# Five feed-forward blocks of an fp32 kernel: two-by-two tile schemes with seven products of 128 tokens in place of eight

## The reference, cut to what matters

```python
def swiglu(y, w_gu, w_down):                    # first network, two per layer
    gate, up = jnp.split(y @ w_gu, 2, axis=-1)  # 1024 x 5632
    return (jax.nn.silu(gate) * up) @ w_down    # 2816 x 1024

def half_ffn(h, m, off, g, w_gu, w_down):
    y = modulate(h, g, m[off], m[off + 1])      # RMS norm, scale, shift
    return h + 0.5 * m[off + 2] * swiglu(y, w_gu, w_down)

ffn = _swiglu(x, w_gate, w_up, w_down)          # second network, one per layer
x = _layer_norm(ALPHA * x + ffn, ln2_g, ln2_b)
```

## Time and profile before

| | |
|---|---|
| time, median of 3 runs | 3701.17 us (3699.54 to 3701.4) |
| the profiled execution's own time | 3700.73 us |
| its span (first to last instruction) | 3698.9 us |
| mean granted TensorE clock | 0.967 of full speed |
| PE / PEld / DVE / ACT / POOL busy | 92% / 74% / 28% / 13% / 5% |
| moved by DMA | 459.40 MB |

### The profile page before, as it was taken

One profiled execution on the slowest core, in us unless ns is written; L12 is line 12 of the kernel. 1 busy time (PEld: TensorE's weight loads), 2 busy tenths in 40 slices (PEclk: granted clock), 3 DMA queues, 4 the chain that ended last, 5 costly groups with the idle time before them and its releaser, 6 DMA issues.

```text
span 3698.9 us, 48516 instructions
## 1 busy us (share of the span) xinstructions
PE 3417.8 (92%) x20808; PEld 2727.1 (74%) x20808; DVE 1039.1 (28%) x1893; ACT 483.1 (13%) x835; POOL 185.1 (5%) x262
## 2 busy tenths in 40 slices
PE   3999989789989899899979999999899899999898
PEld 1444435577878688788858878888788788888787
DVE  5533553455665200100330011322100113321101
ACT  1000010233332100100010000111000001120100
POOL 1000100111111000400000000000000000000000
PEclk7999999999999799999989999999999999999999
DMA  7555742100000144444314455233344343324342
GB/s 279 183 203 181 271 182 89 41 6 6 6 9 2 60 156 136 153 149 158 113 57 149 139 182 175 103 136 128 125 136 139 124 148 113 114 97 171 114 141 97
DMA packets 72129, 459.40 MB, mean 124 GB/s; under 512 B 7632, under 2 KB 10320, under 8 KB 26793
## 3 DMA queue, kind: packets, MB, share of 16 engines
q1 hardware_dynamic: 54720, 362.83, 28.4%
q0 software_dynamic: 12192, 87.03, 6.3%
q10 hardware_dynamic: 5065, 7.27, 0.7%
HBM read 451.34 MB, written 5.77 MB: 124 GB/s over the span
## 4 chain that ended last, share of the span: by engine, by line
PE 88%; DVE 8%; ACT 3%; issue 1%; DMA 1%; DVEq 0%; POOL 0%; ACTq 0%; POOLq 0%
PE ps L531 55%; PE ps L945 12%; PE ps L579 3%; PE ps L541 2%; PE ps L550 2%; PE ps L625 1%; PE ps L631 1%; PE ps L612 1%; DVE arena L1413 1%; DVE arena L1742 1%; PE ps L959 1%; PE ps L1009 1%; PE ps L987 1%; PE ps L672 1%; DVE arena L1627 1%
## 5 line engine op out<-in xcount | busy, mean ns | idle before, releaser
L531 PE MATMUL ps<-y,ring 128*128 128x256 f32 (+1 forms) x3520 | 926.0, 426 | 79.9 <-ACT y L1091 66.9
L531 PEld LDWEIGHTS ps<-y,ring 128*128 128x128 f32 x3520 | 677.2, 193 | 328.9 <-issue 231.7
L531 PE MATMUL ps<-arena,ring 128*128 128x256 f32 (+1 forms) x2624 | 643.3, 408 | 7.7 <-DVE arena L1376 6.0
L531 PEld LDWEIGHTS ps<-arena,ring 128*128 128x128 f32 x2624 | 498.1, 190 | 152.7 <-issue 83.7
L531 PE MATMUL ps<-h,ring 128*128 128x256 f32 x2080 | 460.9, 385 | 19.4 <-ACT h L1340 19.4
L531 PEld LDWEIGHTS ps<-h,ring 128*128 128x128 f32 x2080 | 402.5, 194 | 78.9 <-issue 22.3
L945 PE MATMUL ps<-h,ring 128*128 128x256 f32 x1536 | 343.7, 380 | 0.0
L945 PEld LDWEIGHTS ps<-h,ring 128*128 128x128 f32 x1536 | 289.6, 190 | 41.8 <-issue 2.6
L1376 DVE TENSOR_TENSOR arena<-sg,ps 128x256 f32 (+1 forms) x110 | 46.3, 421 | 735.5 <-ACT sg L1099 735.5
L1413 DVE CUSTOM_DVE_ANT_0 arena<-arena,vec 128x1024 f32<-128x1024 f32 x184 | 224.3, 1281 | 4.4 <-DMA arena<-in_ada_t 4.3
L1099 ACT ACTIVATE sg<-ps 128x256 f32<-128x256 f32 x110 | 42.1, 383 | 701.6 <-PE ps L531 701.6
(11 more groups left out here) (273 smaller groups left out, 2687.4 us busy)
## 6 DMA issues: line engine op xcount, KB each, us to landing
ring<-in_w_f_gu SPq DMA_DIRECT2D x88, 1024.0 KB, 4.8
arena<-in_ada_t POOLq DMA_DIRECT2D x72, 1024.0 KB, 5.2
ring<-in_w_f_down SPq DMA_DIRECT2D x64, 704.0 KB, 4.1
ring<-in_w_fx_gu SPq DMA_DIRECT2D x44, 1024.0 KB, 4.8
ring<-in_w_fx_down SPq DMA_DIRECT2D x32, 704.0 KB, 4.1
ring<-in_w_qk_a SPq DMA_DIRECT2D x18, 1024.0 KB, 4.9
ring<-in_w_qk_r SPq DMA_DIRECT2D x16, 1024.0 KB, 4.9
ring<-in_w_v_r SPq DMA_DIRECT2D x16, 1024.0 KB, 4.9
```

The lines of the kernel that those rows point to most:

```text
L531: last = mm(out, w, rhs_, start=(k == 0 and s.opens), stop=(k == kts - 1 and s.closes))
```

## The change

Each product of a 2 x 2 arrangement of weight tiles with a 2 x 2 arrangement of input halves is rewritten as a Strassen-like scheme. The four weight "quarters" are, in `_gu`, the first and the second half of the input features, for the gate and for the up tile; the input is split into the first and the last 128 tokens. Eight products of a 128 x 128 weight tile with 128 tokens (that is four with 256 tokens) become seven. For this the kernel needs sums of inputs, sums of weight quarters, and sums of the seven results:

- **Weight sums** for every slot: three chained adds and subtractions on POOL (`weight_sums`, 128 x 512 values each, into `w_sums`) and one on DVE (`own_sum`), made two slots ahead of PE.
- **Input sums**: four DVE subtractions of 128 x 512 values after the norm (`input_sums`), and in place of them for the down products four of 128 x 128 values per pair of hidden tiles (`pair_sums`).
- **Products**: 28 matmuls with 128 moving columns per full slot in place of 16 with 256. They lie in seven regions of two PSUM banks. The order is 1, 2, 5, 7, 6, 3, 4: products 1 and 2 need no sums; ahead of product 5 PE waits for `pool_summed` and `dve_summed`.
- **Result sums** (`joined_tiles`): ACT copies region one, and DVE makes five additions from PSUM. In `_gu` the silu and the hidden product follow; the hidden product of a slot (`hidden`) is issued inside the next slot's additions.
- The down stage is cut into 12 slots of 1,024 KB (three for two output tiles, with 4, 4 and 3 pairs of weight tiles) in place of 16 slots of 704 KB: 4 x 77 matmuls.
- The tap matrices are made right after the mixer, three per instruction (31 instructions of 128 x 384), ahead of the weight sums; the transfers of the second network's constants are issued when `o_out` is drained, ahead of the sums for `f2_1`.
- The loops over slots are written out in these blocks (`slots_flat`).

```diff
+    return [(name + "_gu", 22, 1, "quarters", gate_up, l, up), (name + "_down", 12, 3, "quarters_down", down, l, 0)]
...
+            def weight_sums(name):
+
+                for s, stage in seven_slots(name):
+                    n = pairs_of(s, stage)[0]
+                    both, less, rest = (w_sums[:, s.pos, i, 0:n * P] for i in (0, 1, 3))
+                    pool.wait_ge(landed[s.pos], landed_by(stage, s))
+                    nc.gpsimd.tensor_tensor(both, quarter(s, 2, n), quarter(s, 3, n), ALU.add) \
+                        .then_inc(*step(f"pool.both_{s.key}"))
+                    pool.wait_ge(*past(f"pool.both_{s.key}"))
+                    nc.gpsimd.tensor_tensor(less, both, quarter(s, 0, n), ALU.subtract) \
+                        .then_inc(*step(f"pool.less_{s.key}"))
+                    pool.wait_ge(*past(f"pool.less_{s.key}"))
+                    nc.gpsimd.tensor_tensor(rest, quarter(s, 1, n), less, ALU.subtract).then_inc(pool_summed, 1)
+
+            pool.wait_ge(*past(f"dve.mixed{KR - 1}"))
...
+            weight_sums("f2_0")
+            weight_sums("f1_1")
...
+            pool.wait_ge(psum_free, released("f2_1_gu"))
             pool.dma_start(rope, A["rope"]).then_inc(two_in, 16)
...
+            weight_sums("f2_1")
...
+                pool.wait_ge(psum_free, released(f"out{l}"))
+                weight_sums(f"fx_{l}")
...
+                    if s.opens:
+                        pe.wait_ge(psum_free, s.group + 1)
+                    if down and s.group == ST[stage].group:
+                        pe.wait_ge(*past(f"dve.{name}_hid{base + pairs - 1}"))
+                    for number in (1, 2, 5, 7, 6, 3, 4):
+                        if number == 5:
+                            pe.wait_ge(pool_summed, summed_at(s, stage))
+                            pe.wait_ge(dve_summed, summed_at(s, stage))
...
+                        for j in range(pairs):
+                            last = mm(out, weights[number][:, j * P:(j + 1) * P], inputs[number](base + j),
+                                      start=(s.opens and j == 0 and number in (1, 5)), stop=(s.closes and j == pairs - 1),
+                                      skip_group_check=True)
...
+            def own_sum(s, stage):
+                n = pairs_of(s, stage)[0]
+                v.wait_ge(landed[s.pos], landed_by(stage, s))
+                tt(w_sums[:, s.pos, 2, 0:n * P], quarter(s, 0, n), quarter(s, 2, n), ALU.subtract).then_inc(dve_summed, 1)
...
+                v.wait_ge(*past(f"act.{s.key}_one"))
+                tt(quad[:, 2:5:2], quad[:, 7:8].to_broadcast([P, 2, P]), banks[:, 1:3], ALU.add) \
+                    .then_inc(*step(f"dve.{s.key}_one"))
+                extra[0]()
+                v.wait_ge(*past(f"dve.{s.key}_one"))
+                tt(quad[:, 5], quad[:, 4], banks[:, 3], ALU.add).then_inc(*step(f"dve.{s.key}_two"))
+                v.wait_ge(*used)
+                tt(quad[:, 6], quad[:, 4], banks[:, 5], ALU.add).then_inc(*step(f"dve.{s.key}_three"))
+                extra[1]()
+                v.wait_ge(*past(f"dve.{s.key}_three"))
+                tt(quad[:, 3], quad[:, 6], banks[:, 6], ALU.add).then_inc(*step(f"dve.{s.key}_gate"))
+                v.wait_ge(*past(f"dve.{s.key}_two"))
+                tt(quad[:, 0:2], quad[:, 5:6].to_broadcast([P, 2, P]), banks[:, 4:6], ALU.add).then_inc(*closing())
+                extra[2]()
```

More of the change, by code:

```diff
@@ L266, in slots_flat, with hidden_tile, pairs_of, quarter @@
                 yield s
+        def hidden_tile(l):
+            return l // 2 + 11 * (l % 2)
+        def pairs_of(s, name):
+            return (4, 0) if name.endswith("_gu") else (min(4, 11 - 4 * s.half), 4 * s.half)
+        def quarter(s, i, n=4):
+            return ring[:, s.pos, 512 * i:512 * i + n * P]
+        def summed_at(s, name):
+            return 34 * SEVEN.index(name.rsplit("_", 1)[0]) + (22 if name.endswith("_down") else 0) + s.l + 1
+        def seven_slots(name):
+            return [(s, name + part) for part in ("_gu", "_down") for s in slots_flat(name + part)]
         def released(name):
@@ L921, in _ @@
             norm("n5", 1)
-            ffn("f2_1", y1, SEQ)
+            seven("f2_1", y1)
             norm("n6", 1)
@@ L1064, in _ @@
                 layer_norm(f"ln{l}0")
-                ffn(f"fx_{l}", h1, SEQ)
-                pe.wait_ge(psum_free, ST[f"fx_{l}_down"].group + 8 + 2)
+                seven(f"fx_{l}", h1)
+                pe.wait_ge(psum_free, ST[f"fx_{l}_down"].group + 4 + 2)
                 layer_norm(f"ln{l}1")
@@ L1093, in norm, with seven @@
                 last.then_inc(*step(f"act.{name}_y"))
[L1095 to L1099, removed]
+            def seven(name):
+                for s, stage in seven_slots(name):
+                    if stage.endswith("_gu"):
+                        act.wait_ge(slots_used, s.n + 1)
+                    elif s.closes:
+                        act.wait_ge(*past(f"pe.{s.key}_6"))
+                    else:
+                        continue
+                    f(quads[:, s.par, 7], ps[:, 2 * s.par, 0:P], ACT.Copy).then_inc(*step(f"act.{s.key}_one"))
+                    if stage.endswith("_gu"):
+                        act.wait_ge(*past(f"dve.{s.key}_gate"))
+                        f(sg[:, s.par, 0:SEQ], quads[:, s.par, 2:4].rearrange("p a t -> p (a t)"), ACT.Silu) \
+                            .then_inc(*step(f"act.{s.key}"))
             for n, mat in enumerate((ones, blk, ident)):
@@ L1392, in add_gated, with gated, finish, scaled_sum @@
                     last.then_inc(psum_free, 1)
+            def gated(l, which):
+                def finish(item, tiles):
+                    for m in (0, 1):
+                        k = 2 * item + m
+                        last = stt(h[:, 0, k], tiles[:, m], gate[:, l, which, k, 0:1], h[:, 0, k], ALU.mult, ALU.add)
+                    last.then_inc(psum_free, 1)
+                return finish
+            def scaled_sum(item, tiles):
+                hv = h[:, 0, 2 * item:2 * item + 2, :]
+                stt(hv, hv, ALPHA, tiles, ALU.mult, ALU.add).then_inc(psum_free, 1)
             gate_f = gate[:].rearrange("p a b c d -> p (a b c d)")
@@ L2019, in _layout @@
             laid = w.reshape(2, 11, P, KD, P).transpose(3, 0, 2, 1, 4)
+        elif cut == "quarters":
+            other = w[:, :, col:] if isinstance(col, int) else np.asarray(x[col][layer], f).reshape(KD, P, -1)
+            two = np.stack([a[:, :, 0:P * n_slots].reshape(2, 4, P, n_slots, P) for a in (w, other)])
+            laid = two[:, :, :, :, [i // 2 + 11 * (i % 2) for i in range(n_slots)]].transpose(4, 3, 0, 1, 2, 5)
+        elif cut == "quarters_down":
+            two = np.zeros((2, 12, P, D // 256, 2, P), f)
+            two[:, 0:11] = w.reshape(2, 11, P, D // 256, 2, P)
+            laid = two.reshape(2, 3, 4, P, D // 256, 2, P)[:, :, :, :, :, ::-1].transpose(4, 1, 3, 5, 0, 2, 6)
         elif cut == "tall":
```

161 lines of the change are left out of this document (124 added, 37 removed).

## The result

| | before | after |
|---|---|---|
| time, median of the runs compared | 3700.53 us (4 runs) | **3604.41 us** (3601.89 to 3607.51, 4 runs) |
| ratio, with its 95% interval | | 0.9743 [0.9729, 0.9758] |
| the profiled execution | 3700.73 us | 3606.84 us |
| its span | 3698.9 us | 3605.0 us |
| mean granted clock | 0.967 | 0.962 |

The changed kernel is 2.6% faster. The forecast was 3606 us, with a range of 3586 to 3652.

The account below looks back on a forecast made before the run. It took each block to be a dense stream of matmuls on PE. From 3700.73 us: -114.1 for the stream, +6.7 for block tails, +14 for n2 and n5, -0.6 for n3, giving 3606.7, stated as 3606; range 3586 to 3652.

Parts of the forecast that it names:

- The stream: Five blocks: 1,848 records of 128 columns at 112 ns make 207.0 us a block, a gain of 114.1 us.
- first rival: Blocks' matmuls: weight loads don't hide at half the columns, 138 ns a record, 3847 us; chance 0.10.
- PE is fed: Inside the blocks: POOL, DVE and ACT keep up with a 6.27 us slot, so PE never waits and they cost nothing.
- the nearest bound: Gate-up slots: the PSUM buffer must free within 6.27 us; chain 3.95, with one POOL hold 5.0 (expected), two 6.1.
- second rival: Slots with pair sums: three POOL holds make DVE free PSUM in 7.2 us against 6.27, 50 us lost, 3656; chance 0.15.
- n5: Norm ahead of f2_1: POOL's sums run through it and delay DVE's eight products, 7 us lost.
- third rival: Norms n2 and n5: DVE's eight back-to-back products keep POOL out, 14 us less, 3592; chance 0.10.
- n2: Norm ahead of f2_0: after 32 us of taps, POOL's sums run across DVE's eight products, 7 us lost.
- The tails: End of each block: additions and gate products after PE's end grow from 0.48 to some 1.9 us, 6.7 us lost over five.
- the taps in n3: Norm n3: POOL's taps are gone, 1.1 us gained, up to 0.5 given back by POOL's last sums, 0.6 gained.

Follow-up runs that it names:

- experiment 2: The kernel before, with every 256-column product in the five blocks cut into two of 128 and no sums: 3743.61 us, ratio 1.0118.
- experiment 3: The changed kernel without POOL's three weight sums, products 5, 6 and 3 taking plain quarters (output not the reference's): 3592.58 us, ratio 0.9704.
- experiment 4: The changed kernel with POOL's first weight sum made twice, so four chained POOL instructions per slot: 3632.11 us, ratio 0.9815.
- Experiment 7: The changed kernel with POOL's first sum made twice and DVE's own_sum, hidden and pair_sums moved behind the addition that frees PSUM: 3613.86 us, ratio 0.977.
- experiment 1: The changed kernel with POOL's sums held until the products of n2 and n5 and f2_0's last PSUM drain are done: 3592.88 us, ratio 0.9712.
- experiment 5: The changed kernel with 12 spare matmuls on PE behind each block of the first network, into an unused PSUM bank: 3600.31 us, ratio 0.9733.

## Why the prediction was right, step by step

**The stream: right, and the step that carries the result.** The forecast rested on 112 ns for a record of 128 columns, read from two pairs of records in the earlier trace rows. The bounds around it were weaker than they look: half of 216.5 is 108, not 107; four records in 0.39 us are 98 ns each by the rows, not 110; and the 138 of the first rival is a mean. In the trace of before, record by record, L675 and L683 start the next one after 165 ns at 1152 us and every other after 111 or 112, those with 64 columns too but for the first. Over 9,240 records it is 111 or 112 ns; 113 records at half clock (213 or 214 ns) are nearly the only others. The first rival (138 ns, 3847 us) is refuted by the kernel after, and by experiment 2 without any sums around it: 2,112 records per block at the same pace. These fp32 records go from 216.5 to 111.7 ns, a little over half, at half the columns. The Trainium skill, "TensorE: Matmul & The Clock Gate", Back-to-back issue gap, has 81 ns for a bf16 pair whose matmul takes 56; the trace shows hardly any surplus for fp32 (111.7 against 108, half of 216.5), and the measurement decides.

**PE is fed: right, with less to spare than I thought.** No wait for a weight sum occurs. PSUM was named as the nearest bound, with one POOL hold in the chain (5.0 us) and two as the alternative (6.1). The mean is 5.2, but by more holds on a shorter chain: without POOL's sums the buffer comes free in 3.4 us (experiment 3) where the sum of terms said 3.95, and a chain with two holds takes 5.5 (the rows above). One slot in 110 broke it, with four held instructions and 7.0 us. The second rival, DVE too late, is thus not what happens, but it is one POOL instruction away: with a fourth sum per slot it is there and costs 22 us inside the blocks (experiment 4). Its 7.2 us for the chain is near the 7.1 measured by luck: it is four holds on 3.4, not three on 3.95. Experiment 7 shows that the chain is the cause.

**n5: right.** +7.5 for +7. The mechanism is that DVE and POOL exclude each other, and experiment 1 removes it by holding POOL back. The third rival, that back to back products keep POOL out, is refuted by the eleven microseconds of L1468. The Trainium skill, "SBUF — State Buffer", Who interferes with whom, says that these two kinds of instruction block each other in full, and the trace agrees: 1.38 us for a product that takes 0.41 alone.

**n2: right in kind, too high.** The term was 7 and the trace has 1.2, or 1.9 at the norm itself. What failed is the guess that a tap product of 384 columns takes 1.02 us: 27 of them took 21.25 us, 0.79 each. POOL began its sums at 1258.4 in place of 1266 and had finished the four slots before most of the eight products. "POOL's queue is never empty there" was the wrong clause.

**The tails: too low.** The terms were 6.7 - 0.6 = 6.1 for the five, and the trace has 10.8. The longer chain of DVE itself was right, and a little shorter than the term of 1.35: PE's idle time ahead of the norm's sum goes from 1.90 to 3.04 us behind `f1_1` and `f2_1`, and from 0.63 to 1.76 behind `fx_0` and `fx_1`. Two things were missing. The sum's 16 records then ran in part at half clock in the first network, 5.41 us (granted clock 0.68) in place of 3.72 (experiment 5 gives this back), and in `fx` the second sum took 0.7 and 1.1 us more; besides, in n3 POOL was at work on `f1_1` and held up the two gate products (L1589, 2.35 us in place of 0.88). The 1.1 us of the taps in n3 came (L1468 takes 3.26 us there for 4.35), but the 1.5 of L1589 ate it. Behind `f2_1` the mixer that follows gave about 1.4 us back; why is open.

The errors at n2 (5.8 too high) and at the tails (4.7 too low) nearly cancel. With 0.7 us less gained in the blocks and 0.5 more lost in n5, the sum of the terms comes out within 0.1 us of the change of span, and that is luck; the largest term, the stream, and n5 were right by themselves.

Left open: why the clock falls after a 3.04 us wait in one execution and not in the next (see below).

## What to carry to other kernels

Before a scheme that trades products for additions, look for two numbers in the trace: the pace of products of the smaller shape, which decides by itself here (by the forecast's sum 112 ns gains 94 us, and from 122 on the change loses), and the time between an engine's end of a buffer and its release, since the additions' reads stack up there. Put what frees a buffer ahead of the bookkeeping, and keep GpSimd's sums out of stretches where VectorE works alone on the path. A serial stretch that grows can cost more than its length, because the products behind it may run at half clock: here 1.1 us more of waiting often brought 1.7 us more of products.

## What the hardware showed that I had not expected

- **Two engines in strict alternation.** In n5 DVE's products, 0.41 us each when alone (3.26 / 8), come one for each POOL instruction: 11.01 / 8 = 1.38 us, which is POOL's own pace there (1884.72, 1886.13, 1887.41). Neither is starved, and neither gets two turns. POOL pays little: its sums start every 1.34 us alone and every 1.41 here, by the same trace.
- **The clock after an idle wait.** With PE idle for 3.04 us ahead of the norm's sum, its 16 records took 5.41 us behind `f1_1` and `f2_1` in the kernel after (granted clock 0.68 behind `f1_1`) and 3.72 at the same two places in experiment 1 (granted clock 1.00), with 3.03 and 3.04 us idle. In experiment 2 a wait of 1.89 us was enough behind `f2_0`, where 1.90 us before the change, and behind the other two blocks of the same execution, were not. So in this range the length of the wait alone does not decide it. The rows behind `f1_1`, of the kernel after and of experiment 1:

```profile
1714.79 5.41 PE L603 MATMUL ps<-y,ones 128*128 128x256 f32 x16 [3.04 <-ACT y L1169]
...
1711.03 3.72 PE L607 MATMUL ps<-y,ones 128*128 128x256 f32 x16 [3.03 <-ACT y L1173]
```

- **Weight loads overlap each other.** In experiment 2 a weight load of 128 x 128 lasts 192 ns by the trace, and there is one for each product, yet products start every 111.7 ns.
